# Prompt attention of a hybrid decoder layer: who subtracts the spread maximum, from where the maxima are read, and how the PSUM banks are shared

## The reference, cut to what matters

```
s = jnp.einsum('bqhd,bkhd->bhqk', qblk, k).astype(jnp.float32) * ATTN_SCALE
s = jnp.where(kpos[None, :] <= qpos[:, None], s, -jnp.inf)
p = jax.nn.softmax(s, axis=-1).astype(v.dtype)
return jnp.einsum('bhqk,bkhd->bqhd', p, v)
```

## Time and profile before

| | before |
|---|---|
| median of 3 runs | 2058.05 us (2055.15 to 2059.5) |
| the profiled execution's own time | 2060.78 us |
| its span in the trace | 2059.0 us |
| busy share of the span: PE, DVE, ACT, POOL | 94%, 48%, 36%, 27% |
| granted TensorE clock, mean | 0.964 |

### The profile page before, as it was taken

How to read it: one execution, slowest core, us unless ns; L and a number is a source line. 1 busy time by engine, 2 the same in 40 slices (tenths; PEclk the granted TensorE clock), 3 DMA queues, 4 the chain that set the end, 5 groups by cost and what they waited for, 6 DMA issues and landing times. The chain is left out here.

```text
span 2059.0 us, 36182 instructions
## 1 busy us (share of the span) xinstructions
PE 1935.3 (94%) x12672; PEld 1826.8 (89%) x12672; DVE 981.8 (48%) x1591; ACT 750.4 (36%) x1556; POOL 561.1 (27%) x552
## 2 busy tenths in 40 slices
PE   6999997888869999999999699999999999999997
PEld 5999996566649999999998399999999999999997
DVE  6124135688547777777777642323232222223132
ACT  5111224566536666676766332111111111111011
POOL 3232233777710000100000354222222223121221
PEclk8999998999969999999999599999999999999999
DMA  6122000000032222222222111020202111120202
GB/s 218 42 75 63 11 15 14 1 0 0 1 90 63 75 72 72 74 72 75 75 69 109 41 41 53 14 70 21 61 25 56 51 31 52 34 76 6 75 15 100
DMA packets 180603, 108.47 MB, mean 53 GB/s; under 512 B 52132, under 2 KB 177154, under 8 KB 180276
## 3 DMA queue, kind: packets, MB, share of 16 engines
q1 hardware_dynamic: 180358, 107.21, 18.2%
q10 hardware_dynamic: 174, 0.30, 0.1%
HBM read 97.47 MB, written 10.00 MB: 52 GB/s over the span
## 5 line engine op out<-in xcount | busy, mean ns | idle before, releaser
L1911 PE MATMUL banks<-comb_hi,pageT_hi 128*128 128x272 f32 x1024 | 234.1, 310 | 0.0
L1801 DVE TENSOR_REDUCE k_sums<-k_sq 128x8 f32<-128x512 f32 x256 | 174.4, 681 | 91.9 <-ACT k_sq L1619 91.9
L2268 DVE TENSOR_TENSOR xT<-xT,banks 128x1074 f32<-128x1074 f32 x64 | 81.6, 1274 | 276.7 <-PE banks L244 276.7
L1911 PE MATMUL banks<-comb_hi,pageT_lo 128*128 128x272 f32 x1024 | 212.4, 289 | 0.0
L1911 PE MATMUL banks<-comb_lo,pageT_hi 128*128 128x272 f32 x1024 | 212.0, 288 | 0.0
L1619 ACT ACTIVATE k_sq<-banks 128x512 f32<-128x512 f32 x256 | 152.1, 594 | 141.9 <-PE banks L1911 139.0
L233 POOL TENSOR_TENSOR w_down_lo<-w_down_raw,w_down_hi 128x512 fp32r<-128x512 f32 x64 | 95.0, 1484 | 346.6 <-ACT w_down_hi L229 346.6
L2150 ACT ACTIVATE a_hi<-relu 128x1074 fp32r<-128x1074 f32 x32 | 35.4, 1105 | 396.0 <-DVE relu L2256 396.0
L233 POOL TENSOR_TENSOR w_out_up_lo<-w_out_up_raw,w_out_up_hi 128x1024 fp32r<-128x1024 f32 x40 | 101.8, 2554 | 273.7 <-ACT w_out_up_hi L229 273.7
L244 PE MATMUL banks<-hf_hi,w_out_up_hi 128*128 128x358 f32 x768 | 169.5, 329 | 0.0
L244 PE MATMUL banks<-a_hi,w_down_lo 128*128 128x358 f32 x768 | 169.1, 328 | 0.0
(11 more groups left out here) (382 smaller groups left out, 4078.5 us busy)
## 6 DMA issues: line engine op xcount, KB each, us to landing
page_latents<-in_cache_kv_latent SPq DMA_DIRECT2D x256, 128.0 KB, 2.1
w_out_up_raw<-in_w_up SPq DMA_DIRECT2D x32, 512.0 KB, 4.2
w_down_raw<-in_w_down SPq DMA_DIRECT2D x64, 256.0 KB, 2.7
w_in_raw<-in_w_in SPq DMA_DIRECT2D x17, 512.0 KB, 3.9
x_spill<-xT SPq DMA_DIRECT2D x1, 4296.0 KB, 15.0
xT<-x_spill SPq DMA_DIRECT2D x1, 4296.0 KB, 13.9
page_ropes<-in_cache_k_rope SPq DMA_DIRECT2D x256, 16.0 KB, 1.7
w_out_up_raw<-in_w_o SPq DMA_DIRECT2D x8, 512.0 KB, 4.4
```

The source lines that it names most:

```text
L1801: nc.vector.tensor_reduce(ksum[par][:, j, :], sq[j % 2][:, :].rearrange("p (h c) -> p h c", h=H), AX_X, ALU.add)\
L1911: mm = pe.matmul(banks[:, 2 * (j % 2) + half, 0:WC], x[j % AHEAD][:, k, :], w[par][:, k, half, :], start=k == 0 and a == 0, stop=k == KL - ...
L2268: nc.vector.tensor_add(x, x, slot(s)[:, :, 0:TB]).then_inc(down.evacuated[s], 1)
```

## The change

VectorE takes over the subtraction from GpSimd (`shift`). It reads the spread maximum from PSUM where TensorE left it, so ScalarE's copy of it (`keep_spread`) and its SBUF tiles are gone, and the spread maxima have two PSUM banks (4 and 5) in place of one. Bank 5 was the third score bank, so the score blocks go round two banks. `maxima` reads the new block in its PSUM bank and only the other side from SBUF; so a score bank comes free when ScalarE's copy and VectorE's maximum are both done, and `score` of block j waits for both of block j-2. VectorE keeps the reciprocals of the sums (`invert_sums`, now at the end of a go), and GpSimd multiplies with them (`norm_pair`). On VectorE the shift stands at the start of a go, ahead of the maxima, and `find_max` of the next head's first chunk stands ahead of `split_lo`. In the code `keep_output` of the second chunk moves from the start of the next iteration to the end of its own.

```diff
-    spread = [ar.take(f"max_spread{i}", [P, 400], F32) for i in range(2)]
-    SCORE_BANKS = (0, 1, 5)
-    SPREAD_BANK, TURN_BANK, UNIT_BANK = 4, 6, 7
+    TURN_BANK, UNIT_BANK = 6, 7
     MAX_STEPS = (8, 12, 14)
+    STEPS_AFTER = (0, 1, 2, 3, 4, 7, 8, 8, 9, 11, 12, 14)
-    def spread_of(par, c):
-        return spread[(par + c) % 2]
+    def spread_bank(par, c):
+        return 4 + (par + c) % 2
...
-            def shift(n, par, go):
-                for j in (2 * go, 2 * go + 1):
-                    c = CHUNK_OF[j]
-                    pool.wait_ge(s["max_copied"], n * NC + (c + 1))
-                    for k, q0, q1, at in parts(j):
-                        x = S[par][0:keys_of(k), at:at + q1 - q0]
-                        a = q0 - CHUNKS[c][0]
-                        done = nc.gpsimd.tensor_sub(x, x, spread_of(par, c)[0:keys_of(k), a:a + q1 - q0])
-                done.then_inc(s["shifted"], 1)
...
+            def norm_pair(pair, c):
+                q0, q1 = CHUNKS[c]
+                pool.wait_ge(s["sums_inverted"], pair * (2 * NC) + (2 * c + 2))
+                x = g.attnT[:, ds(pair, 1), q0:q1].rearrange("p o t -> p (o t)")
+                nc.gpsimd.tensor_mul(x, x, g.sums[:, q0:q1]).then_inc(s["normed"], 1)
...
-            def keep_spread(n, par, c):
-                w = CHUNKS[c][1] - CHUNKS[c][0]
-                act.wait_ge(s["max_spread"], n * NC + (c + 1))
-                ge(act, s["shifted"], n * GOES + LAST_GO[0] if c == 2 else n * GOES)
-                act.copy(spread_of(par, c)[:, 0:w], banks[:, SPREAD_BANK, 0:w]).then_inc(s["max_copied"], 1)
...
+                    here, out = banks[0:m, j % 2, a:a + q1 - q0], top[0:m, q0:q1]
+                    if x > 0 or not begun:
+                        v.wait_ge(s["max_steps"], n * MAX_STEPS[-1] + done)
+                    if first and x == 0:
+                        nc.vector.tensor_scalar(out, here, 1.0, None, ALU.mult).then_inc(s["max_steps"], 1)
+                    elif begun and x == 0:
+                        nc.vector.tensor_max(out, src[:, start_of[j - 1]:start_of[j - 1] + width[j]], here).then_inc(s["max_steps"], 1)
                     else:
-                        v.wait_ge(s["max_steps"], n * MAX_STEPS[-1] + done)
-                    nc.vector.tensor_max(top[0:m, q0:q1], top[0:m, q0:q1] if a is None else src[0:m, a:a + w], src[0:m, b:b + w]).then_inc(s["max_steps"], 1)
+                        nc.vector.tensor_max(out, out, here).then_inc(s["max_steps"], 1)
...
+            def shift(n, par, go):
+                for j in (2 * go, 2 * go + 1):
+                    c = CHUNK_OF[j]
+                    v.wait_ge(s["max_spread"], n * NC + (c + 1))
+                    for k, q0, q1, at in parts(j):
+                        x = S[par][0:keys_of(k), at:at + q1 - q0]
+                        a = q0 - CHUNKS[c][0]
+                        done = nc.vector.tensor_sub(x, x, banks[0:keys_of(k), spread_bank(par, c), a:a + q1 - q0])
+                done.then_inc(s["shifted"], 1)
...
-                ge(pe, s["copied"], n * NB + (j - 2))
-                bank = SCORE_BANKS[j % 3]
+                ge(pe, s["copied"], n * NB + (j - 1))
+                ge(pe, s["max_steps"], n * MAX_STEPS[-1] + (STEPS_AFTER[j - 2] if j >= 2 else STEPS_AFTER[j - 2] - MAX_STEPS[-1]))
+                bank = j % 2
...
-                ge(pe, s["max_copied"], n * NC + c)
-                pe.matmul(banks[:, SPREAD_BANK, 0:q1 - q0], g.ones[:, :], diag[:, 0:q1 - q0], start=True, stop=True)\
+                ge(pe, s["shifted"], n * GOES + LAST_GO[0] if c == 2 else n * GOES)
+                pe.matmul(banks[:, spread_bank(par, c), 0:q1 - q0], g.ones[:, :], diag[:, 0:q1 - q0], start=True, stop=True)\
```

More of the change, by code:

```diff
@@ L1111, in loop @@
                 for go in range(GOES):
-                    if have(n, 0) and go < GOES - 1:
-                        shift(n, par, go + 1)
                     if have(n, 0) and go < 2:
                         diagonal(n, 1 + go)
+                    if norm and go % 2 == 1:
+                        norm_pair(pair - 1, go // 2)
                     if have(n, 1) and go == 2:
@@ L1147, in keep_scores @@
                 ge(act, s["pv_done"], n * NB - 2 * NB + (j + 1))
-                act.copy(S[par][:, start_of[j]:start_of[j] + width[j]], banks[:, SCORE_BANKS[j % 3], 0:width[j]]).then_inc(s["copied"], 1)
-            def keep_spread(n, par, c):
-                w = CHUNKS[c][1] - CHUNKS[c][0]
-                act.wait_ge(s["max_spread"], n * NC + (c + 1))
-                ge(act, s["shifted"], n * GOES + LAST_GO[0] if c == 2 else n * GOES)
-                act.copy(spread_of(par, c)[:, 0:w], banks[:, SPREAD_BANK, 0:w]).then_inc(s["max_copied"], 1)
+                act.copy(S[par][:, start_of[j]:start_of[j] + width[j]], banks[:, j % 2, 0:width[j]]).then_inc(s["copied"], 1)
             def probabilities(n, par, go):
@@ L1175, in loop @@
                 for go in range(GOES):
-                    if have(n, -1) and go == 0:
-                        keep_output(n - 1, 1 - par, before, 1)
                     if have(n, 1):
@@ L1194, in loop @@
                         probabilities(n + 1, 1 - par, 0)
+                    if go == GOES - 1 and have(n, 0):
+                        keep_output(n, par, pair, 1)
                 if isinstance(n, int) and n == H - 1:
-                    keep_output(n, par, pair, 1)
                     keep_output(n, par, pair, 2)
@@ L1247, in maxima @@
                     return done
[L1248 to L1260, removed]
-                    else:
-                        v.wait_ge(s["max_steps"], n * MAX_STEPS[-1] + done)
-                    nc.vector.tensor_max(top[0:m, q0:q1], top[0:m, q0:q1] if a is None else src[0:m, a:a + w], src[0:m, b:b + w]).then_inc(s["max_steps"], 1)
+                begun = first or done == ((0,) + MAX_STEPS)[c]
@@ new lines, in maxima @@
+                if begun:
+                    ge(v, s["max_transposed"], n * NC - NC + (c + 1))
+                for x, (k, q0, q1, at) in enumerate(blk):
+                    m, a = keys_of(k), at - start_of[j]
+                    here, out = banks[0:m, j % 2, a:a + q1 - q0], top[0:m, q0:q1]
[5 more added lines that the diff above has]
+                        nc.vector.tensor_max(out, src[:, start_of[j - 1]:start_of[j - 1] + width[j]], here).then_inc(s["max_steps"], 1)
+                    else:
+                        nc.vector.tensor_max(out, out, here).then_inc(s["max_steps"], 1)
@@ L1269, in norm_pair, with invert_sums @@
+            def invert_sums(pair, go):
                 c, half = go // 2, go % 2
@@ L1275, in norm_pair @@
                 nc.vector.reciprocal(g.sums[:, cols], g.sums[:, cols]).then_inc(s["sums_inverted"], 1)
[L1276 to L1279, removed]
             def loop(n, par, pair, norm):
@@ L1286, in loop @@
                 for go in range(GOES):
-                    if norm:
-                        norm_pair(pair - 1, go)
+                    if have(n, 0) and go < GOES - 1:
+                        shift(n, par, go + 1)
                     if have(n, 1):
@@ L1293, in loop @@
                         find_max(n, 1 + go)
+                    if have(n, 1) and go == 4:
+                        find_max(n + 1, 0)
                     if have(n, 2) and go < NU:
                         split_lo(n + 2, par, go)
-                    if have(n, 1) and go == 4:
-                        find_max(n + 1, 0)
+                    if norm:
+                        invert_sums(pair - 1, go)
+                    if have(n, 1) and go == GOES - 1:
+                        shift(n + 1, 1 - par, 0)
             loops(v, loop)
```

13 lines of the change are left out of this document (3 added, 10 removed).

## The result

The changed kernel takes 2024.9 us (median of 4 runs, 2023.75 to 2026.15) beside 2056.6 for the kernel before in the same session: a ratio of 0.984, 95% interval 0.9826 to 0.9853. That is 31.7 us less; 28 were forecast, and the time lies in the range.

A forecast was written before the change was run, and what follows sets the result against it. TensorE, with the most work but idle 3 to 7 us per iteration, was taken as the bound, VectorE in normalising iterations; 26.2 + 4.8 - 2.8 = 28.2, rounded to 28 us less, forecast 2030 us, range 2016 to 2050.

The forecast's parts named there:

- VectorE's prices: Subtraction or maximum with one side in PSUM: 0.56 us at 400 columns; per head 7.3 us of subtractions, 6.2 of maxima.
- The allowance for such overlaps: On VectorE, instructions that wait for nothing start about 0.08 us early; over some twenty places, 1.8 us back.
- Two causes: TensorE waits 14.0 us at turns behind GpSimd's late subtraction, 9.9 and 4.1 for `split_lo` behind maxima held up by GpSimd.
- Light and heavy iterations: Iterations 0 to 6: four light at 22.4 us, two heavy (normalising a pair) at 26.3, iteration 6 at 23.0.
- the wait for the second unit: At the turn TensorE waits up to 1.0 us for the second unit from ScalarE's line, where it waited 0.6.
- The last head: Final head of the stage: 19.14 us falls to 14.3 with 1.5 of waits left, 4.8 us less.
- The clock allowance of 2.8 us: Set against the gain: two light iterations keep TensorE's reduced clock, at 1.4 us each.
- The ring of two score banks: Rival: score banks and VectorE's in-order list close a ring, 5.0 us a go; 14 us slower, 2072 us; chance 0.09.
- the chain at the turn: ScalarE's line where heads change, from the subtraction to the second unit: 4.8 us, 5.1 with hand-overs.
- VectorE the bound everywhere: Rival: VectorE's in-order list waits for ScalarE's copies each go; light iterations 25.5 us, 12 us less, 2046; chance 0.20.
- Everything closing up: Rival: light iterations at 21.4 us, heavy at 24.3, iteration 6 at 21; 41 us less, 2017; chance 0.06.
- No measurable effect: Rival: VectorE pays back in subtraction what it gains in maxima, ScalarE's line binds the turn; no measurable change; chance 0.05.

The follow-up runs named there:

- two small edits to it: The changed kernel with reciprocals spread over the pair and ScalarE's output copies of the middle chunk ahead of the exponential: 2011.1 us, ratio 0.9774.

## Why the prediction came out right, point by point

**VectorE's prices held.** 400-column subtractions and maxima read from PSUM take 0.55 to 0.57 us (0.56 forecast), the maxima 6.2 us a head (6.2). The subtractions occupy 50.0 / 8 = 6.25 us rather than 7.3: their records overlap, 128 of 445 ns would be 57. The allowance for such overlaps, 1.8 us an iteration, was too small: in iteration 2 VectorE's groups by line add up to 25.5 us, and VectorE is busy 22.71, where 24.3 were forecast. So heavy iterations took 25.26 us and not 26.3, although VectorE idled 2.55 us in each and not 2. The Trainium skill's page "VectorE: DVE Perf Modes", section on the TRN2 errata, would have each of these cost 0.065 us more (an estimate, worked out ahead of the result). No run here shows that surcharge: a two-sided maximum that nothing holds up takes 562 ns at 400 columns in the run that moves only the subtraction, beside L1244's 563 in the changed kernel.

**Two causes were named, and their weights were not.** That GpSimd's subtraction is late at the turn, and that GpSimd's work holds up two-sided maxima, are both shown. The held-up maxima are the larger cause: read from PSUM in the kernel before, they give 1.2% of the 1.6% alone, and without the PSUM side everything else keeps 0.7%. The subtraction alone gives 0.2%. On top of the maxima the rest of the change gives 0.4%, some 8 us, and the turn's wait falls from 12.6 to 5.4 us; where the maxima keep both sides in SBUF, the held-up ones ahead of the turn keep that wait at 12.8 to 15.5. How the 0.4% divides between the subtraction on VectorE and ScalarE's copy of the spread maximum, which goes with it, no run shows: none keeps the copy while the maxima read PSUM. In the run of the maxima alone the copy stands in the chain of a turn for 0.57 us (407.09 to 407.66), an estimated 4 us in seven turns if nothing hides it.

**Light and heavy iterations**: 22.07 us on average (22.4 forecast) and 25.26 (26.3), iteration 6 22.33 (23.0). The iterations gave 30.3 us, not 26.2. The light ones came out near the forecast by other terms than its own: TensorE's own work in iterations 1, 3 and 5 is 21.4 to 22.0 us rather than 21.1, and the wait for the second unit, put at 1.0 in each, is 1.5 in all. The wait for the diagonal came out as forecast (1.7 us in all, 0.2 a head), and with `find_max` late again it is 6.4. That heavy ones are bound by VectorE is shown by the runs that fill its gap or spread its reciprocals.

**The last head is the term that was mis-sized**: 3.0 us less where 4.8 were forecast. The step "with 1.5 us of waits left it takes 14.3" left out the 2.23 us for the output copies: TensorE idles 3.33 us in that window and not 1.5. Its 12.8 us of own work came out at 12.78 by luck, at a clock of 0.89 and not at full clock; with the copies ahead of the exponential the same head has 11.13 us of work at 1.00, and takes 13.38.

**The clock allowance of 2.8 us was not needed**: 1.00 in all seven iterations. It added to the low estimate of their gain, 26.2 for 30.3, so that these two terms lie 6.9 us under the trace; the last head's 1.8 too much took some of that back. The traces give 33.3 us for the terms that the forecast put at 28.2, and the medians, 31.7 apart, lie nearer to it: that the number came so close is in part luck.

**The output copies.** The move in the code leaves them behind the exponential in both kernels; that it changes nothing no run tests apart. But a place ahead of the exponential was worth 10 us, and I had read the chain at the turn ("exponential 0.87, output copies 0.95, two score copies 0.87") without asking whether its order was needed.

**The rivals.** VectorE the bound everywhere: no, light iterations are 3 us shorter than heavy ones. The ring of two score banks: `score` waits 0.7 us in all; with one bank less of cover the loss is 102 us, so the mechanism is real and two banks are enough. Everything closing up (2017) was not what this change did, but 2011 was within reach of two small edits to it. No measurable effect: no, the interval ends at 0.9853.

## What to carry to other kernels

Look at the longest record of a line, not only its mean: here a VectorE operation with both sides in SBUF that took many times its shortest of the same shape was held up by GpSimd, and reading one side where it already lay in PSUM was worth more than moving GpSimd's work. Then look at the order of what an in-order engine does where the loop turns: an engine that idles ahead of a step while later work of its own is ready can lose that time for everybody behind it. And try such parts alone and on top of each other: the subtraction alone gave 6.2 us here, and the part of the change that it belongs to gave 8 on top of the maxima.

## What the runs showed that I had not expected

The hold-up can last through several GpSimd instructions: with two-sided maxima in the changed kernel a 384-column one, 0.56 us in the changed kernel at the same place, took 3.66 us and ended 0.41 us after a gapless run of three. Not every one lasts so long: in the kernel before, many maxima of 1.1 to 1.6 us ended while GpSimd's next instruction was already running. What decides between the two is not shown. The page "SBUF — State Buffer" of the Trainium skill, section "Who interferes with whom", says that the two contend; this length is the trace's.

TensorE's granted clock magnified waits. In the kernel with one bank of cover the first scores, 344.70 to 377.15 us, run at 0.50, the lower of its two levels throughout, and take 32.5 us; in the changed kernel 344.70 to 360.80 is granted 0.88 and takes 16.1. The fall itself is not the difference: in both the clock goes to 0.50 between 330 and 335 us, around which TensorE idles 1.4, 1.1 and then 7.4 us for other engines. What differs is the rise. In the changed kernel TensorE works from 344.82 to 354 us without a wait, and the clock is 1.00 from 350 us on; with one bank of cover it waits 0.4 to 1.3 us for a copy or a maximum ahead of nearly every block, and the clock stays at 0.50 until about 385 us.
